# A two-block transformer kernel: the up projections of its plain layers as seven half-size products

## The reference, cut to what matters

```python
def swiglu_ffn(x, w_gate, w_up, w_down):            # the gated layers: ffn0, ffn1
    return (jax.nn.silu(x @ w_gate) * (x @ w_up)) @ w_down

def sq_relu_mlp(h, w_up, w_down):                    # the plain layers: mlp0, mlp1
    u = jax.nn.relu(h @ w_up)                        # h: 512 x 1024, w_up: 1024 x 4096
    return (u * u) @ w_down                          # w_down: 4096 x 1024

# each plain layer: h = h + sq_relu_mlp(rmsnorm(h, ln_mlp[layer]), w_up[layer], w_down[layer])
```

## Time and profile before

| | before |
|---|---|
| median of three runs | 2398.31 us |
| the profiled execution's own time | 2398.89 us |
| its span in the trace | 2397.1 us |
| TensorE busy | 2357.7 us (98%), 12574 matmuls |
| VectorE busy | 1670.5 us (70%) |
| ScalarE busy | 999.6 us (42%) |
| DMA, mean share of its 16 engines | about 28%; 96 GB/s |

### The profile page before, as it was taken

The page is one execution under the profiler, slowest core; times in us unless marked ns, Lnnn a source line. Parts: engine busy times, 40 slices in busy tenths (PEclk is TensorE's granted clock), DMA queues, the critical chain, the costliest instruction groups (busy, mean ns, idle before and its releaser), DMA issues.

```text
span 2397.1 us, 30288 instructions
## 1 busy us (share of the span) xinstructions
PE 2357.7 (98%) x12574; PEld 1989.9 (83%) x12574; DVE 1670.5 (70%) x2234; ACT 999.6 (42%) x1414; POOL 22.7 (1%) x39
## 2 busy tenths in 40 slices
PE   8999999999999999999999999999999999999998
PEld 7887888899998887899998786888888777888886
DVE  5998746887778746888778636566556786666566
ACT  4446444544444734544445525322212565222122
POOL 0000000000000000000000000000000000000000
PEclk9999999999999999999999999999999999999999
DMA  5322313232233212233223220333333212222321
GB/s 185 105 91 104 119 40 106 88 103 94 104 106 116 90 52 71 88 106 106 92 103 111 88 103 21 105 105 122 108 125 107 87 54 71 92 102 88 106 94 65
DMA packets 38872, 228.96 MB, mean 96 GB/s; under 512 B 8837, under 2 KB 8917, under 8 KB 12496
## 3 DMA queue, kind: packets, MB, share of 16 engines
q1 hardware_dynamic: 31680, 219.17, 26.2%
q0 software_dynamic: 7056, 7.86, 1.4%
HBM read 221.71 MB, written 5.24 MB: 95 GB/s over the span
## 4 chain that ended last, share of the span: by engine, by line
PE 84%; DVE 8%; ACT 5%; issue 1%; DMA 1%; SPq 0%; DVEq 0%; ACTq 0%
PE bank L779 83%; DVE w_lo L2221 2%; ACT w_hi L1583 1%; DMA w_raw<-weights_in 1%; ACT xs L1676 1%; ACT xh L1614 1%; DVE xl L2244 1%; DVE cacc L2550 1%; PE bank L1516 1%; DVE xs L2359 0%; DVE xs L2339 0%; DVE traw L2391 0%; DVE tl L2396 0%; ACT pr L1953 0%; ACT xs L1740 0%
## 5 line engine op out<-in xcount | busy, mean ns | idle before, releaser
L779 PE MATMUL bank<-xh,w_hi 128*128 128x512 f32 (+1 forms) x1248 | 440.4, 353 | 14.2 <-DVE w_lo L2772 7.2
L779 PE MATMUL bank<-xl,w_hi 128*128 128x512 f32 (+1 forms) x1248 | 435.7, 349 | 0.0
L779 PE MATMUL bank<-xh,w_lo 128*128 128x512 f32 (+1 forms) x1248 | 435.5, 349 | 0.0
L2221 DVE TENSOR_TENSOR w_lo<-w_raw,w_hi 128x2048 fp32r<-128x2048 f32 x138 | 316.2, 2291 | 166.4 <-ACT w_hi L1583 166.3
L1583 ACT ACTIVATE w_hi<-w_raw 128x2048 fp32r<-128x2048 f32 x138 | 263.3, 1908 | 263.0 <-PE bank L779 257.2
L2315 DVE TENSOR_TENSOR xs<-xs,bank 128x512 f32<-128x512 f32 x448 | 292.5, 682 | 65.3 <-PE bank L779 64.8
L779 PEld LDWEIGHTS bank<-xh,w_hi 128*128 128x128 f32 x1248 | 236.7, 190 | 54.3 <-DVE w_lo L2772 7.2
L779 PEld LDWEIGHTS bank<-xh,w_lo 128*128 128x128 f32 x1248 | 236.7, 190 | 30.6
L779 PEld LDWEIGHTS bank<-xl,w_hi 128*128 128x128 f32 x1248 | 236.8, 190 | 29.8 <-issue 0.5
L779 PE MATMUL bank<-yh,w_hi 128*128 128x512 f32 x576 | 227.3, 395 | 0.2 <-DVE w_lo L2221 0.2
L779 PE MATMUL bank<-yl,w_hi 128*128 128x512 f32 x576 | 224.3, 389 | 0.0
(11 more groups left out here) (325 smaller groups left out, 4294.6 us busy)
## 6 DMA issues: line engine op xcount, KB each, us to landing
w_raw<-weights_in SPq DMA_DIRECT2D x204, 1024.0 KB, 4.9
rel_scratch<-vt POOLq DMA_DIRECT2D x8, 384.0 KB, 20.1
bias<-rel_scratch POOLq DMA_DIRECT2D x8, 256.0 KB, 3.1
y_out<-xs SPq DMA_DIRECT2D x8, 256.0 KB, 2.2
xs<-x_in SPq DMA_DIRECT2D x3, 512.0 KB, 9.3
mk<-mem_in POOLq DMA_DIRECT2D x1, 1024.0 KB, 8.9
window<-consts_in POOLq DMA_DIRECT2D x1, 576.0 KB, 4.1
xs<-x_in SPq DMA_DIRECT2D x2, 256.0 KB, 4.5
```

Source lines behind the costliest of these rows:

```text
L779: return pe.matmul(dst, a, b, start=start, stop=stop, skip_group_check=adds)
L2221: dve.tensor_tensor(w_lo[:, ring(c)], w_raw[:, c % 2, :], w_hi[:, ring(c)].bitcast(F32), ALU.subtract)\
```

## The change

It has three parts. (1) In the plain layers the 16 chunks become 8 pairs of chunks. The two up units of a pair (except pair 0) are computed as seven products, as in the gated layers. The squares are taken before the factor of the norm, so the hidden tile is multiplied by `rstd` squared (`r2`) behind them. The weight sums lie in `yraw_sums`, the differences come from `yraw`, an fp32 copy of the scaled input that ScalarE now makes. (2) The down projection of a pair sums 512 hidden rows in a bank, so there are eight additions to `xs` for two chunks instead of sixteen. (3) At the entry of the gated layers ScalarE scales `xs` before it splits S1, and VectorE makes S2 earlier and the low part of T4 later. POOL's DMAs of the bias table are tied to the new items.

```diff
@@ planning @@
-MLP_CHUNKS = 4096 // 256
+MLP_PAIRS = 4096 // 512
...
+def mlp_up(name, c, second):
+    return UNITS[name] + (4 * c - 2 if c else 0) + second
+def mlp_down(name, c, half):
+    return UNITS[name] + (4 * c + 4 if c < MLP_PAIRS - 1 else 4 * c + 2) + half
...
+    def quarters_of(name, c):
+        for h in range(2):
+            for q in range(2):
+                item((name, c, f"d{h}{q}"), 1)
+            RELEASE[mlp_down(name, c, h)] = ITEM[name, c, f"d{h}1"] + 1
+
+    def pieces_of(name, c, a, b):
+        for piece in PIECES:
+            item((name, c, piece), 1)
+        RELEASE[a] = ITEM[name, c, "S2" if c == 1 else "S1"] + 1
+        RELEASE[b] = ITEM[name, c, "b1"] + 1
@@ POOL @@
-                pool.wait_ge(unit_used, ITEM[UNITS["mlp0"] + 3 + 2 * g])
+                pool.wait_ge(unit_used, ITEM["mlp0", 1 + g // 2, ("a0", "b1")[g % 2]])
...
-                pool.wait_ge(unit_used, ITEM[UNITS["mlp0"] + 20 + g])
+                pool.wait_ge(unit_used, ITEM["mlp0", 5 + g // 4, ("a0", "S1", "S4", "b1")[g % 4]])
@@ TensorE, mlp @@
+                def down(c):
+                    hh, hl = (mhh, mhl) if c < MLP_PAIRS - 1 else (zhh, zhl)
+                    for half in range(2):
+                        for q in range(2):
+                            key = (name, c, f"d{half}{q}")
+                            pe.wait_ge(w_lo_ready, ITEM[key] + 1)
+                            if half == 0:
+                                pe.wait_ge(sem["h_ready"], 2 * (chunk_base[name] + c) + q + 1)
+                            for m in range(4 * half, 4 * half + 4):
+                                if q == 0:
+                                    wait_free(pe, (name, c, "d", m))
+                                for k in range(2):
+                                    last = mm3(bank((name, c, "d", m))[:, :], piece(key, k * 512 + m % 4 * P),
+                                               (hh[:, q, k, :], hl[:, q, k, :]), q == 0 and k == 0, q == 1 and k == 1)
...
+                up_unit(name, 0, 0, mlp_up(name, 0, 0), ytile, ready)
+                up_unit(name, 0, 1, mlp_up(name, 0, 1), ytile)
+                for c in range(1, MLP_PAIRS):
+                    seven_products(name, c)
+                    down(c - 1)
@@ ScalarE, residual and ffn @@
                         square(k, xs[:, k, :])
+                        if gain:
+                            give(act.activation(yraw[:, k, :], xs[:, k, :], ACT.Copy, scale=col(gain, k)), "y_raw")
...
-                hi_of_piece(name, 1, "S1")
-                high_of_h(name, 0)
                 for k in range(KT):
                     last = act.activation(xs[:, k, :], xs[:, k, :], ACT.Copy, scale=ALPHA)
                 give(last, "scaled_ready")
+                hi_of_piece(name, 1, "S1")
+                high_of_h(name, 0)
@@ VectorE, sums @@
+            def s_raw(name, c, which):
+
+                ua, a0 = raw_of(name, c, "a0")
+                ub, b0 = raw_of(name, c, "b0")
...
+                if which == "S1":
+                    dve.wait_ge(raw_loaded[ua % 2], 16 * (ua // 2 + 1))
+                    dve.wait_ge(raw_loaded[ub % 2], 16 * (ub // 2 + 1))
@@ VectorE, mlp, entry @@
+                split_lo(mlp_up(name, 0, 1))
+                t_raw(name, "T1")
+                t_raw(name, "T2")
+                t_low(name, "T1")
+                t_raw(name, "T3")
+                t_raw(name, "T4")
+                seen.next("rstd_ready")
+                steps.step(dve.tensor_tensor(r2, rstd[:, :], rstd[:, :], ALU.mult))
+                first_hidden(0)
+                lo_of_piece(name, 1, "a0")
+                lo_of_piece(name, 1, "a1")
+                t_low(name, "T2")
+                s_raw(name, 1, "S1")
+                s_raw(name, 1, "S3")
+                squared(0, 0)
+                s_raw(name, 1, "S2")
+                lo_of_piece(name, 1, "S1")
+                first_hidden(1)
+                s_raw(name, 1, "S4")
+                t_low(name, "T3")
+                squared(0, 1)
+                low_of_hidden(0, 0)
@@ VectorE, mlp, a pair @@
+                for c in range(1, MLP_PAIRS):
+                    more = c + 1 < MLP_PAIRS
+                    if c > 1:
+                        add_down(c - 2, 7)
+                    lo_of_piece(name, c, "S2")
+                    if c == 1:
+                        t_low(name, "T4")
+                    low_of_hidden(c - 1, 1)
+                    lo_of_piece(name, c, "S4")
...
+                    quarter(mh, name, c, "a", sum_x, 0, 0)
+                    lo_of_piece(name, c, "S3")
+                    lo_of_piece(name, c, "b1")
+                    lo_of_piece(name, c - 1, "d00")
...
+                    lo_of_piece(name, c - 1, "d11")
+                    squared(c, 1)
+                    by_token(1)
+                    if more:
+                        add_down(c - 1, 0)
+                        s_raw(name, c + 1, "S1")
+                        lo_of_piece(name, c + 1, "a0")
+                        add_down(c - 1, 1)
+                        s_raw(name, c + 1, "S3")
...
```

More of the change, by code:

```diff
@@ L272, in mlp, with last_of_half @@
     def mlp(name):
-        def last_of(c):
-            return lambda m: mlp_down(name, c) if m == KT - 1 else None
         first = 2 * side(UNITS[name])
[L277 to L281, removed]
+        bank_of = {0: first, 1: first + 1, 2: 2 - first, 3: 3 - first}
+        def last_of_half(c):
+            return lambda m: (name, c, f"d{m // 4}1") if m % 4 == 3 else None
+        for second in range(2):
+            plain_up(name, 0, second, mlp_up(name, 0, second), bank_of[2 * second])
+        for c in range(1, MLP_PAIRS):
+            for part, b, piece in PRODUCTS:
+                fill((name, c, part), bank_of[b], (name, c, piece))
+            downs(name, c - 1, last_of_half(c - 1))
+        downs(name, MLP_PAIRS - 1, last_of_half(MLP_PAIRS - 1))
     pairs("ag0", 1), pairs("a0", 1), pairs("ag1", 1), pairs("f", 2)
@@ L461 @@
     "s_raw",
+    "y_raw",
     "u3_ready",
@@ L627, in build @@
         swa_mem = ExitStack()
+        yraw = sb(alias, "yraw", [P, KT, T])
+        alias.close()
+        yraw_sums = sb(alias, "yraw_sums", [P, 4, UNIT // 2])
+        alias.close()
+        zhh = sb(alias, "zhh", [P, 2, 2, T], F32R)
+        zhl = sb(alias, "zhl", [P, 2, 2, T], F32R)
+        alias.close()
         sf = sb(swa_mem, "sf", [P, KT * T])
@@ L1244, in mlp @@
             def mlp(name, ready):
[L1246 to L1260, removed]
+                def down(c):
[12 more added lines that the diff above has]
+                                               (hh[:, q, k, :], hl[:, q, k, :]), q == 0 and k == 0, q == 1 and k == 1)
+                                if q == 1:
+                                    full(last, (name, c, "d", m))
+                            if q == 0:
+                                last.then_inc(unit_used, 1)
+                up_unit(name, 0, 0, mlp_up(name, 0, 0), ytile, ready)
+                up_unit(name, 0, 1, mlp_up(name, 0, 1), ytile)
+                for c in range(1, MLP_PAIRS):
+                    seven_products(name, c)
                     down(c - 1)
-                down(MLP_CHUNKS - 1)
+                down(MLP_PAIRS - 1)
             def first_ready(k):
@@ L2413, in quarter @@
-                def quarter(c, part, with_, which, t0):
-                    key = (name, c, part)
-                    wait_full(dve, key)
-                    free(dve.tensor_tensor(gu[:, which, :, t0:t0 + 256], halves(bank(key)[:, :]), halves(with_[:, :]), ALU.add), key)
                 def low_of_h(c):
@@ L2497, in mlp, with add_down, squared @@
             def mlp(name):
-                def up(chunk):
-                    split_lo(mlp_up(name, chunk) + 1)
+                r2 = sq[:, 1, :]
+                def add_down(c, m):
+                    add(m, (name, c, "d", m))
+                def squared(c, j):
+                    h = mh[:, j, :, :]
+                    if c:
+                        for part in ("a", "y2") if j == 0 else ("z3", "b"):
+                            wait_drained(dve, (name, c, part))
+                    else:
+                        for m in range(2):
+                            wait_drained(dve, (name, 0, j, m))
+                    ins = dve.scalar_tensor_tensor(h, h, 0.0, h, ALU.max, ALU.mult)
+                    if c:
+                        steps.step(ins)
+                    else:
+                        ins.then_inc(sem["hf_ready"], 1)
@@ L3087, in pack_weights @@
         out[f"ffn{l}"] = in_chunks((i["ffn_wg"][l], i["ffn_wu"][l]), i["ffn_wd"][l])
-        out[f"mlp{l}"] = in_chunks((i["w_up_2"][l],), i["w_down_2"][l])
+        u = wide(i["w_up_2"][l])
+        d = i["w_down_2"][l].reshape(MLP_PAIRS, 4, P, 2, D // 2).transpose(0, 3, 2, 1, 4).reshape(-1, P, UNIT)
+        order = [u[0:2]]
+        for c in range(MLP_PAIRS):
+            order += [u[2 * c + 2:2 * c + 4], d[2 * c:2 * c + 2]]
```

(1 more changed line is left out.)

336 lines of the change are left out of this document (210 added, 126 removed).

## The result

| | before | after |
|---|---|---|
| median of the runs, us | 2398.44 (2395.65 to 2398.73, 4 runs) | 2436.03 (2433.68 to 2437.86, 4 runs) |
| ratio, 95% interval | | 1.0158 [1.0145, 1.0171] |
| profiled execution: its time, span | 2398.89, 2397.1 | 2436.73, 2435.0 |
| mean granted clock | 0.997 | 0.987 |

A forecast was written before the change was run, and what follows sets the result against it. TensorE, busy in 98% of the span, was taken as the bound. Terms -22.5 - 8.7 + 11.8 + 44 = +24.6 on the profiled 2398.89 us gave 2423 us, range 2377 to 2437.

The forecast's parts named there:

- Products instead of plain units: Plain layers' up units: seven products per pair save 1.61 us in each of 14 pairs, 22.5 us saved.
- VectorE's halved additions: Plain layers' down projection: half the additions into `xs`, costed at nothing because VectorE is not the bound.
- The gated entries: Entry of both gated layers: reordering removes a 2.78 us gap and 1.58 us of half clock each, 8.7 us saved.
- The tightest margin: Gated entry: S1's low half is made at 440.8, against 441.57 when it is needed.
- The plain entries: Entry of both plain layers: S1 0.3 us late, S2 4.0, plus 1.6 of clock; 5.9 us each, 11.8 us lost.
- Pairs 1 to 4: First plain layer: loads late beside bias-table stores hold addition 1 and so TensorE; 8.9 + 3 x 11.7 = 44 us lost.
- The second layer and pairs 5 to 7 whole: Second plain layer and the first's pairs 5 to 7: all VectorE work in time, no TensorE gaps, 41.9 us per pair.
- Margins of 0.3 us: Steady pair in the plain layers: loads and additions all in time, by 0.3 us at the least.
- loads in time: Rival B, pairs 1 to 4: S1's load still lands by about 30, none of the 44 us comes; 2379.5 us, chance 0.22.
- Half the wait: Rival C, pairs 1 to 4: S1's load takes 7.5 us, 6.8 us lost four times; 2406.6 us, chance 0.14.
- Too tight in every pair: Rival E: VectorE's margins cost each of 14 pairs up to 1 us, 14 more; chance 0.07 shared with D.

The follow-up runs named there:

- without stores: Changed kernel without POOL's eight stores of the bias table's rows, the bias loads reading weights instead: 2381.19 us, ratio 0.9921 to the kernel before.
- the stores were spread: Changed kernel with the same eight bias-table stores copied from DRAM with 128 outermost, over all 16 DMA engines: 2381.88 us, ratio 0.9925.
- the additions first: Changed kernel with VectorE's sums S1, S3, S2, S4 of the next pair behind additions 0 to 3 instead of between them: 2399.69 us, ratio 1.0002.
- the stores at d10: Changed kernel with both bias-table stores of a pair issued at once at the start of d10, not at a0 and b1: 2417.06 us, ratio 1.0074.

## Why the prediction was right

Slower was forecast, by the mechanism that the runs show, and 2436 lies inside the range, at its upper end. Only sizes were off. In the order of the prediction's terms:

- **Products instead of plain units: -22.5, measured -22.5.** Seven products take 20.15 us and a whole pair 20.15 + 21.79 = 41.94. In this trace the 120 and 227 ns of the earlier trace rows hold; with 109 and 216 ns a pair would be 39.05, 2.9 us shorter. The Trainium skill ("TensorE: Matmul & The Clock Gate", section "Back-to-back issue gap") gives these two by a formula that it calls the gap of an isolated matmul and not of a stream of weight loads and matmuls, so they were no price for this stream. VectorE's halved additions were put at nothing; no run takes them apart.
- **The gated entries: -8.7, measured -7.9 in the change and -8.3 alone.** No gap stands there. The tightest margin that I named, S1's low half, held.
- **The plain entries: +11.8, measured +4.9 and +5.8 = 10.7.** Both gaps are there, but split otherwise. TensorE's timeline at the first layer's entry:

```profile
1556.88 0.35 PE L832 MATMUL bank<-xh,w_hi 128*128 128x256 f32 x1 [0.80 <-DVE mh L2645]
1563.06 0.39 PE L832 MATMUL bank<-xh,w_hi 128*128 128x256 f32 x1 [3.08 <-DVE w_lo L2332]
```
  S1 starts 1.0 us late and not 0.3, and its releaser is `mh`, the reading of a hidden tile out of the bank that S1 writes to, where I had followed only the low half. S2 starts 3.2 us late and not 4.0. The half clock, counted twice, came once: behind the same gap the granted clock of the next 3.44 us is whole in the first layer and averages 0.55 in the second.

```profile
1563.06:1566.50 3.44, 3.17 (x25) 2.97 (x25) 3.44 (x4) 2.84 (x5) 0.00 (x0) 1.00 0.75 236
2114.06:2117.50 3.44, 3.44 (x17) 3.44 (x18) 3.44 (x4) 2.57 (x4) 0.00 (x0) 0.55 0.68 229
```
- **Pairs 1 to 4: +44, measured +56.8.** This is the step with the wrong size, and the term in it that is furthest off is the load of d10's unit, which I put at 9.7 us, between the two landings of the earlier trace rows. In pairs 2 to 4 it took 13.2, 12.8 and 12.5. The load for S1, put at 12.2, took 11.2 to 12.9. Both are in the chain of the second pair above (1620.78 and 1639.25).

  In my schedule of pair 2 (its products start at 1609.12) d10's unit lands at 21.5; it landed at 24.9. S1's lands at 39.2; it landed at 41.4. TensorE resumed 2.2 us later than forecast (44.5 against 42.3), and this down projection lost 13.8 us instead of 11.7: the same 2.1. With an offset of 11.3 us from the store, between 4.1 (landing 12.4) and 17.3 (landing 7.5), I had drawn a straight line through two points. What the trace has in its place is the end of the store: in pairs 2 to 4 the store was under way for 22.0 to 22.4 us, not 19.9, and d10's unit landed 2.4, 1.9 and 1.3 us behind its end. In pair 1, beside a store of 18.5 us, it was asked for 12.0 us behind it, landed 2.5 us behind its end, and so took only 9.0. The far bound, both loads at 12.4, was 58 us, and would have been the better value.

  With d10's unit later than about 22, addition 0 is late as well, and tile 4 has a gap of its own (1.3 to 2.0 us in pairs 2 to 4), of which the prediction says nothing. It makes the restart later by nothing, since tile 5 waits longer anyway.

  Another part of the step is the clock. Behind the restart it was half for 5.6, 3.4, 4.5 and 5.9 us in pairs 1 to 4, so 2.8, 1.7, 2.3 and 3.0 us are lost, 9.8 in all where the prediction has four times 1.6: 3.4 of the 12.8 us between 44 and 56.8.
- **The second layer and pairs 5 to 7 whole: right.** Margins of 0.3 us held, except in the first down projection of the first layer (0.6 us lost without stores).

The sum, in rounded terms: 12.8 us for the pairs, -1.1 for the plain entries, +0.8 for the gated ones, and 0.6 at the end of the layer make the 13 us between forecast and result.

The rivals: *loads in time* (2379.5) is what came when the stores were spread (2381.88). It had the right price for a stage without this contention, and was wrong on whether the contention reaches the late loads. *Half the wait*, to which the Trainium skill's rule on turns between transfers ("DMA: Bandwidth & Descriptors", section "Queues, rings and completion order") had pointed, did not occur: the loads for S1 and, in pairs 2 to 4, those of d10's unit took 11 to 13 us. The trace does not bear out what I made of that rule, a load that waits for one turn: in the packets above the load's last two sixteenths had none for 3.2 us and came as the store ended. *Too tight in every pair* fell with the run without stores.

## What to carry to other kernels

An in-order engine that empties a matmul's banks must have nothing ahead of that work which waits for a load, unless the load has its worst landing time in hand, and the worst is to be read beside whatever else is on the DMA engines then. That holds for every such item: in the run with the additions first, one low half left between two of them still held tile 5 in two pairs, and these were 11.2 us too long. A DMA that broadcasts from two partitions can be small in bytes and long in time (here 384 KB and 22 us): give it a form that spreads it, before anything near it is made tighter. A wait that costs nothing before a change (here loads of 7.5 us in the median, up to 12.5) is the first thing to price when the change takes away the cover.

## What had not been expected of the hardware

- A store of 384 KB out of two partitions took 22.1 us and held loads of 1 MB at 10.3 us in the median; written from DRAM with 128 outermost, the same bytes took 4.6 us and the loads 4.8.
- The same gap of 3.36 us in TensorE's stream, at the entry of a plain layer, was followed by very different clocks. In the first layer of the changed kernel and of the run without stores the clock stayed whole, and from the restart to the down projection it took 12.14 us. In the second layer of the changed kernel 3.4 us were at half clock, and it took 13.10. In the second layer of the run without stores, and in the first of the runs with the stores spread, the additions first and the stores at d10, 5.7 to 6.0 us were at half clock, and it took 14.1 to 14.3. A gap of this length is thus worth between 0 and 2.1 us more than itself, and from the traces I cannot tell which beforehand.
- Of the long records of half clock around the 10-us gaps (up to 13.7 us) most lies in the idle time and costs nothing. What costs is the part behind the restart, in the second and in the fourth pair these:

```profile
1653.60:1657.04 3.44, 3.44 (x8) 2.76 (x9) 3.44 (x5) 0.00 (x0) 0.00 (x0) 0.50 0.02 5
1767.15:1773.10 5.95, 5.95 (x14) 4.69 (x15) 5.68 (x6) 0.00 (x0) 0.00 (x0) 0.50 0.00 0
```
  In the second 3.44 us are at half clock and 1.7 lost, about the 1.6 that the prediction had taken from the gated entry; in the fourth 5.95 us, and 3.0 lost.
